# Neighbourhood attention of a two-stack kernel: the column mask built into the shifted bias table by its transfers, in place of an addition on GpSimd

## The reference, cut to what matters

```python
def neighborhood_attn(q, k, v, rpb):          # rpb (H=4, 15, 31)
    rows = s // GRID_W                        # 256 positions = 4 rows x 64 columns
    kh = min(NA_KH_MAX, rows)                 # 4: every query sees all 4 rows
    scores = einsum(q, k) * d ** -0.5
    c0 = clip(c - NA_KW // 2, 0, GRID_W - NA_KW)          # NA_KW = 16
    col_ok = (c[None, :] >= c0[:, None]) & (c[None, :] < c0[:, None] + NA_KW)
    dc = clip(c[None, :] - c[:, None], -15, 15) + 15
    bias = rpb[:, dr][..., dc]
    scores = where(col_ok, scores + bias, NEG_INF)
    p = softmax(scores)
    return einsum(p, v)
```

## Time and profile before

| what | value |
|---|---|
| median of 3 runs | 1360.22 us (1356.76 to 1361.85) |
| the profiled execution's own time | 1358.29 us |
| its span in the profile | 1356.4 us |
| TensorE busy | 1298.9 us, 96% |
| VectorE busy | 989.3 us, 73% |
| ScalarE busy | 696.6 us, 51% |
| GpSimd busy | 279.2 us, 21% |
| DMA, mean share of 16 engines | 56% |
| TensorE's mean granted clock | 0.992 |

### The profile page before, as it was taken

One profiled execution on the slowest core, in us unless ns is written; L12 is line 12 of the kernel. 1 busy time (PEld: TensorE's weight loads), 2 busy tenths in 40 slices (PEclk: granted clock), 3 DMA queues, 4 the chain that ended last, 5 costly groups with the idle time before them and its releaser, 6 DMA issues.

```text
span 1356.4 us, 21347 instructions
## 1 busy us (share of the span) xinstructions
PE 1298.9 (96%) x8100; PEld 1156.5 (85%) x8100; DVE 989.3 (73%) x1172; ACT 696.6 (51%) x952; POOL 279.2 (21%) x253
## 2 busy tenths in 40 slices
PE   3989999998999999999999999999999999999997
PEld 3988898987888888998888888888889898888886
DVE  2697769778776677866766777866776876776776
ACT  3476556645444459554544445444447664544443
POOL 2465247437100012311000005500002410100000
PEclk9999999998999999999999999999999999999999
DMA  8843374355666655424666665766655434666661
GB/s 228 237 157 125 125 208 135 125 152 158 199 188 187 186 156 155 124 95 124 204 190 191 189 184 154 206 190 191 188 158 154 128 111 123 182 191 186 186 190 57
DMA packets 273070, 224.38 MB, mean 165 GB/s; under 512 B 17780, under 2 KB 255735, under 8 KB 272870
## 3 DMA queue, kind: packets, MB, share of 16 engines
q1 hardware_dynamic: 268448, 217.08, 53.5%
q10 hardware_dynamic: 3958, 4.27, 1.0%
q0 software_dynamic: 592, 2.04, 0.9%
HBM read 222.25 MB, written 3.08 MB: 166 GB/s over the span
## 4 chain that ended last, share of the span: by engine, by line
PE 80%; DVE 10%; issue 3%; ACT 3%; DMA 2%; POOL 0%; ACTq 0%; DVEq 0%; POOLq 0%; SPq 0%
PE wide L1550 24%; PE wide L1551 12%; PE big L1513 8%; PE big L1515 8%; PE big L1514 7%; PE wide L1513 5%; PE wide L1514 5%; PE wide L1515 5%; DVE w_lo L833 3%; PE wide L1804 2%; DMA w_raw<-in_w_in 1%; PE wide L1657 1%; ACT w_hi L441 1%; DVE work L1033 1%; DVE proj L889 1%
## 5 line engine op out<-in xcount | busy, mean ns | idle before, releaser
L833 DVE TENSOR_TENSOR w_lo<-w_raw,w_hi 128x2048 fp32r<-128x2048 f32 x205 | 487.3, 2378 | 101.2 <-ACT w_hi L441 100.3
L1550 PE MATMUL wide<-h_both,w_hi 128*128 128x512 f32 x1408 | 500.8, 400 | 0.0
L441 ACT ACTIVATE w_hi<-w_raw 128x2048 fp32r<-128x2048 f32 x206 | 393.6, 1911 | 201.8 <-PE big L1515 133.1
L1551 PE MATMUL wide<-h_both,w_lo 128*128 128x256 f32 x1408 | 396.2, 281 | 0.0
L1550 PEld LDWEIGHTS wide<-h_both,w_hi 128*128 128x128 f32 x1408 | 265.7, 189 | 65.6 <-DVE w_lo L833 0.2
L1551 PEld LDWEIGHTS wide<-h_both,w_lo 128*128 128x128 f32 x1408 | 267.0, 190 | 1.4
L1513 PE MATMUL wide<-h_both,w_hi 128*128 128x256 f32 x720 | 210.2, 292 | 10.0 <-DVE w_lo L833 6.3
L1514 PE MATMUL wide<-h_both,w_hi 128*128 128x256 f32 x720 | 205.4, 285 | 0.0
L1515 PE MATMUL wide<-h_both,w_lo 128*128 128x256 f32 x720 | 205.2, 285 | 0.0
L1513 PE MATMUL big<-w_hi,y_hi 128*128 128x512 f32 x480 | 190.3, 396 | 0.0
L1515 PE MATMUL big<-w_hi,y_lo 128*128 128x512 f32 x480 | 187.8, 391 | 0.0
(11 more groups left out here) (235 smaller groups left out, 1520.9 us busy)
## 6 DMA issues: line engine op xcount, KB each, us to landing
w_raw<-in_w_in SPq DMA_DIRECT2D x112, 512.0 KB, 4.7
w_raw<-in_ffn_w_gate SPq DMA_DIRECT2D x88, 512.0 KB, 4.0
w_raw<-in_ffn_w_up SPq DMA_DIRECT2D x88, 512.0 KB, 5.2
w_raw<-in_ffn_w_down SPq DMA_DIRECT2D x88, 512.0 KB, 4.2
w_raw<-in_w_out SPq DMA_DIRECT2D x32, 512.0 KB, 4.3
work<-rpb_shifted SPq DMA_DIRECT2D x32, 64.0 KB, 4.2
rpb_shifted<-rpb_rows POOLq DMA_DIRECT2D x1, 1920.0 KB, 25.9
cst<-in_consts ACTq DMA_DIRECT2D x1, 1063.0 KB, 6.9
```

The source lines that it names most:

```text
L441: nc.scalar.activation(w_hi[:, r, :], w_raw[:, r, :], ACT.Copy).then_inc(hi_ready, 1)
L833: v.tensor_tensor(w_lo[:, r, :], w_raw[:, r, :], w_hi[:, r, :].bitcast(F32), ALU.subtract).then_inc(lo_ready, 1)
L1550: t_.matmul(o, a_hi, h_both[:, kt].rearrange("p a s -> p (a s)"), start=first, stop=False, skip_group_check=True)
L1551: return t_.matmul(o[:, 0:S], a_lo, h_hi[:, kt, :], start=False, stop=last, skip_group_check=True)
```

## The change

The padded table gets two rows ("variants") of 128 numbers for each of the 120 raw rows, filled with the large negative number in place of zero. Variant 0 holds only the 16 middle numbers of the raw row, variant 1 all 31. The shifted table is then built by five transfers in place of one: the 49 middle query columns come from variant 0, so that their 16-wide window is surrounded by the negative number; for the first 8 and the last 7 query columns the 16 key columns of the window come from variant 1 and the other 48 from a piece of padding. Together the five write the same 1,966,080 bytes. GpSimd's addition L1422 and its two waits go, the mask's 64 columns leave the constants, and VectorE waits for the landing of the 16 transfers of its layer (`bias_in`) itself.

```diff
@@ constants()
-    col = np.arange(P) % GRID_W
-    c0 = np.clip(col - NA_KW // 2, 0, GRID_W - NA_KW)[:, None]
-    kc = np.arange(GRID_W)[None, :]
-    c[:, C_NA:C_NA + GRID_W] = np.where((kc >= c0) & (kc < c0 + NA_KW), 0.0, NEG)
@@ stacks_kernel()
-        padded = y_f[0:DEPTH * NH * RPB_ROWS, 0:P]
+        padded = y_f[0:DEPTH * NH * RPB_ROWS, 0:2 * P].rearrange("n (a c) -> n a c", a=2)
-        scratch = nc.dram_tensor("rpb_rows", (DEPTH * NH * RPB_ROWS, P), F32)
+        scratch = nc.dram_tensor("rpb_rows", (DEPTH * NH * RPB_ROWS, 2, P), F32)
@@ VectorE
-                            dve.wait_ge(bias_ready, l + 1)
+                            dve.wait_ge(bias_in, l * 256 + 256)
                             soft(un, u, na_bias[:, u - 2])
@@ GpSimd
-            link(g.memset(padded, 0.0))
-            pool.dma_start(padded[:, 48:48 + RPB_COLS],
-                           a["na_rpb"].rearrange("l h r c -> (l h r) c")).then_inc(rpb_a, 16)
-            pool.wait_ge(rpb_a, 16)
+            half = NA_KW // 2
+            table = a["na_rpb"].rearrange("l h r c -> (l h r) c")
+            link(g.memset(padded, NEG))
+            pool.dma_start(padded[:, 0, 63 - half:63 + half], table[:, RPB_COLS // 2 - half:RPB_COLS // 2 + half]).then_inc(rpb_a, 16)
+            pool.dma_start(padded[:, 1, 48:48 + RPB_COLS], table).then_inc(rpb_a, 16)
+            pool.wait_ge(rpb_a, 32)
             pool.dma_start(scratch.ap(), padded).then_inc(rpb_b, 16)
             pool.wait_ge(rpb_b, 16)
 
-            pool.dma_start(shifted, bass.AP(scratch, 63, [[P, DEPTH * NH * RPB_ROWS], [-1, GRID_W], [1, GRID_W]])
-                           ).then_inc(rpb_a, 16)
+            def band(at, step, rows_, cols):
+                return bass.AP(scratch, at, [[2 * P, DEPTH * NH * RPB_ROWS], [step, rows_], [1, cols]])
+
+            right, last = GRID_W - half + 1, GRID_W - NA_KW
+            for dst, src in (
+                    (shifted[:, half:right, :], band(63 - half, -1, right - half, GRID_W)),
+                    (shifted[:, 0:half, 0:NA_KW], band(P + 63, -1, half, NA_KW)),
+                    (shifted[:, 0:half, NA_KW:], band(0, 0, half, last)),
+                    (shifted[:, right:, last:], band(P + 63 - right + last, -1, half - 1, NA_KW)),
+                    (shifted[:, right:, 0:last], band(0, 0, half - 1, last))):
+                pool.dma_start(dst, src).then_inc(rpb_a, 16)
             norm(0)
...
-            pool.wait_ge(rpb_a, 32)
+            pool.wait_ge(rpb_a, 16 * 7)
             pool.sem_inc(shifted_ready, 1)
...
                     if (c, j) == (0, DVE_TAPS):
-                        pool.wait_ge(bias_in, l * 256 + 256)
-                        nb = na_bias.rearrange("p t h (a b) -> p (t h a) b", b=GRID_W)
-                        g.tensor_tensor(nb, nb, cst[:, C_NA:C_NA + GRID_W].unsqueeze(1).to_broadcast([P, 32, GRID_W]),
-                                        ALU.add).then_inc(bias_ready, 1)
                         pool.wait_ge(conv_part, l + 1)
                         pool.sem_inc(pool_step, 1)
```

More of the change, by code:

```diff
@@ L93 @@
 B_A, B_L1M, B_C1, B_KS, B_ALL = 8, 12, 16, 20, 24
-C_ID, C_ROT1, C_SWAP, C_ROT2, C_COS, C_SIN, C_SWA, C_FOX, C_DIL, C_NA, C_FREQ, C_FXB, NCONST = (
-    0, 128, 256, 384, 512, 768, 1024, 1536, 2048, 2560, 2624, 2626, 2638)
+C_ID, C_ROT1, C_SWAP, C_ROT2, C_COS, C_SIN, C_SWA, C_FOX, C_DIL, C_FREQ, C_FXB, NCONST = (
+    0, 128, 256, 384, 512, 768, 1024, 1536, 2048, 2560, 2562, 2574)
 FXR = 16
@@ L267, in stacks_kernel @@
         bias_in = sem("bias_in")
-        bias_ready = sem("bias_ready")
         par_T = sem("par_T")
```

## The result

| | before | after |
|---|---|---|
| median | 1359.61 us (1356.76 to 1361.85, 6 runs) | 1350.04 us (1349.21 to 1350.76, 6 runs) |
| ratio, with 95% interval | | 0.9926 (0.9916 to 0.9936) |
| the profiled execution's own time | 1358.29 us | 1350.72 us |
| its span | 1356.4 us | 1348.8 us |
| TensorE busy | 1298.9 us | 1296.3 us |

The change is faster by 0.74%, some 10 us. I had forecast 1.9 us less and called a gain above 0.5% a case of 1 in 10: the forecast, its range (1353.5 to 1365.5) and its chances were wrong. The two profiled executions are 7.6 us apart.

A forecast was written before the change was run, and what follows sets the result against it. It took VectorE as the limit early on, with TensorE waiting behind it. Gains of 2.4 + 1.7 + 0.35 = 4.4 us less 2.5 us for the transfers gave 1.9 us less, 1358.3 us; range 1353.5 to 1365.5 us.

The forecast's parts named there:

- The price of the addition: Both layers: GpSimd's mask addition stalls VectorE's subtraction, 6.66 in place of 2.28 us; removal gives VectorE 4.4 us back.
- 2.4 + 1.7: First layer, TensorE at unit 2: 2.4 us of waiting for exponentials goes, and 1.7 us of low clock behind it.
- In the second layer only 0.35 us of waiting stand at this place: Second layer, TensorE's wait at the same place: removal gains only 0.35 us, though VectorE gains 4.4 us there too.
- fourth rival: Whole kernel: earlier work escapes further low-clock stretches, two on top of the whole 4.4 us, giving 1352.5 us; chance 0.10.
- The new transfers: Start of the kernel: the five table transfers cost 2.5 us, 1.7 for more pieces plus 0.8 for another issue.
- what the table takes longer I count in full: Start: a later table delays the weights that VectorE's chain hangs on, so all of 1.7 + 0.8 us counts.
- A line through both has 14.9 ns for a piece and the rest for its bytes: Table transfers at the start: piece price from two queues' shares, making 1800 more pieces 1.7 us of every engine.
- The scratch doubles to 120 KB, but in as many pieces; I put that at nothing: Scratch at the start: 60 KB more are 0.2 us at 264 GB/s, so counted as nothing.
- below, it may be nothing or 1 us of gain: Start: lower bound of the transfers' cost, if short pieces spread the load of the engines better.
- the second rival: Start: tables dealt to 15 engines in place of 16, landing at 34.1 us, 9.0 us lost, 1364.8 us; chance 0.17.
- the transfers cost nothing: Start: time goes with bytes, which stay the same, so the 4.4 us come whole, 1355.8 us; chance 0.20.
- The gain not taken: Behind the exponentials another wait ends as late, so only the start's 2.5 us loss remains, 1362.7 us; chance 0.08.

The follow-up runs named there:

- no_mask: Kernel before with only GpSimd's mask addition taken away, so the bias goes unmasked and the table is built as before: 1353.59 us, ratio 0.9956.
- scratch_144: Kernel before with scratch rows 576 bytes apart in place of 512, table still one transfer of 7680 rows: 1354.3 us (1 run).
- changed_again: The changed kernel run once more, nothing altered: 1349.99 us, ratio 0.9921 against the kernel before.
- by_layer: Changed kernel with the second layer's tables built during the first layer by five more transfers: 1350.34 us, ratio 0.9925 against the kernel before.
- scratch_doubled: Kernel before with scratch rows 1024 bytes apart in place of 512, table still one transfer of 7680 rows: 1369.73 us (1 run).
- two_of_3840: Kernel before with its table built by two transfers of 3840 rows in place of one of 7680: 1352.95 us (1 run).
- the last variants: Changed kernel with the two scratch variants in separate blocks, rows 512 or 576 bytes apart: 1349.81 and 1349.13 us.
- transfers_only: Changed kernel with the mask addition and the mask's constants put back: 1356.41 us, ratio 0.9971 against the kernel before.

## Why the prediction was wrong

**The price of the addition: right in mechanism, and right in size for the first layer.** "The subtraction has stood still behind the addition": 6.66 us became 2.28, and with the addition put back into the changed kernel it is 6.67 again. "2.4 + 1.7" for the first layer was 4.1, and `no_mask` measured 4.06. The Trainium skill's page "SBUF — State Buffer", section "SBUF: two separate sides", has a shared port pair that a GpSimd operation, or a VectorE operation with two inputs in SBUF against a GpSimd one that reads SBUF, holds for the whole instruction if it starts first, while the other is fully blocked. The traces agree: the addition started 0.05 us ahead, and 2.1 us are left from its end to the subtraction's.

**The second layer: undersized.** The step "In the second layer only 0.35 us of waiting stand at this place" took one wait as the whole effect. It measured 2.07 us. The low clock at 230 to 234 us stood in the trace before, and ended some 16 us ahead of the wait that I read (249.1 us); it had made TensorE late by itself. A wait is what is left after both sides' delays; where the side that waits has been slowed too, the wait is a lower bound. The prediction's fourth rival (the clock gives more, 0.10) named this kind of thing, and its 1352.5 us was the nearest of the five numbers, but it named no place.

**The new transfers: wrong sign, the main error.** The term said +2.5 us. Measured on the mark of GpSimd's first operation it is -4.0 us, and in time -3.9 us. The failed step is the one from the engines' time to the delay: "what the table takes longer I count in full", with the 25.9 us of the landing taken as what these bytes and pieces need in any form. The engines' time was nearly the same, 22.1% for q0 against 21.6%, 0.3 us of every engine more, and the table was still done 6.0 us earlier (33.2 against 39.2 us), because the tail of few packets was gone.

The price of a piece, "A line through both has 14.9 ns for a piece and the rest for its bytes", was worked out from a share that held 99 slow packets, so it isn't a price of small pieces as such. With the 13.8% of the same 7680 pieces in `scratch_144` the same formula gives 0.138 x 16 x 55 / 7920 = 15.3 ns for 258 bytes in place of 24.0, the line through that and the 46.6 ns for 898 bytes has 2.7 ns for a piece, and the 1.7 us of the term become 0.3. Neither is what the runs show for 1800 more pieces at a like form, 1.8 us at 512 bytes and 0.8 at 576. And no such price gives the right sign: with 0.3 in place of 1.7 the term is still +1.1 us.

"The scratch doubles to 120 KB, but in as many pieces; I put that at nothing": with the one transfer it cost 9.3 us of time (1369.73 against 1360.48 us beside it, one run, whose profiled start is 10.0 us later at the convolution), more than any other single edit here moved the time. In the change its harm was outweighed by the split into five.

What I did see right was whom it would hit: "what the table takes longer I count in full", on SyncE's hanging issue. The same path carried the gain: 12.12 us of hanging became 2.98. And the sentence "below, it may be nothing or 1 us of gain" set the lower bound too narrow. The table's 25.9 us called for a bound of its own on this side: had it landed in half the time, up to 12 us of a hanging issue would have come free. I only weighed slower forms for it (the second rival: 34.1 us), never a quicker one.

**The rivals.** That the transfers cost nothing (0.20) fell on the good side of it: they gave. That the table goes to fewer engines (0.17) fell by its own condition: the packets under way level off at 15 in the kernel before as after, so nothing changed there. The Trainium skill's page "DMA: Bandwidth & Descriptors", section "Why a DMA increments its semaphore by 16 and not by 1", takes the largest number up to 16 that divides the outermost counts of both sides. The packets agree: before, the destination has 7680 rows but the source 120, which gives 15. That the change would move it from 16 to 15 was my misreading, since I took the destination alone. The estimate of 6.5 us from that page's section "Anatomy of one DMA" still isn't reached: the quickest form of all 1920 KB in one transfer took 12.6 us. The gain not taken (0.08) was wrong.

**Where the profile's 7.6 us stand to this.** The removal's 4.1 and 2.1 us of `no_mask` and the start's 4.0 would be 10.2 in all, near the medians' 9.6, but no single profile shows that sum. In the profiled execution of the changed kernel the first layer gave only 1.73 of its 4.06 us. TensorE came to unit 0 earlier than VectorE and ScalarE did, waited 2.1 and not 1.5 us, and the low clock at 92 to 97 us followed. That isn't chance of one execution: the profile of `changed_again` has the same stretch at 0.66 and the same span, 1348.8 us. So part of the start's gain is given back inside the first layer, as in `by_layer`. The 2.0 us between the profiles' 7.6 and the medians' 9.6 are the 1.3 us by which the profiled execution of before was faster than its median and the 0.7 by which that of the changed kernel was slower.

**By the list of what would show it.** The subtraction at 2.3 us: came true. The wait before unit 2 and its low clock gone: came true. Unit 0's wait "stays near 1.5 us but lies 2 to 3 us later, because the weights of slot 4 land at 50 to 51 us": wrong, ScalarE takes the same weights up at 43.72 us where it was 48.05. The text said that the start's part would be wrong if the half slot's issue ended before 39.8 us, and it did, at 31.1 us.

**What stays open.** Why the packets of one form of transfer slow down, and why a few of them make a tail. The distance between the rows read matters (576 bytes against 512 against 1024), the split matters, and the distance of the tables written matters in the one transfer (25.9 to 12.6 us) but not in the five (13.4 to 13.5). The records of the packets name no engine and no place in memory. A rival is untested: `scratch_144` and `scratch_doubled` also make the scratch longer, so the tables behind it may have begun at another address, and no run moves them with the distance kept. `two_of_3840` shows only that the addresses of before don't by themselves make the table slow. Whether the 1 to 2 us between the spans of the last variants are real is open too.

## What to carry to other kernels

When a transfer from DRAM to DRAM takes much longer than its bytes, count it as a fault that an innocent edit may mend or worsen, and put the mended case into the range; here 64 bytes more between the rows read took the landing from 25.9 to 12.7 us. Its share of the engines doesn't tell its delay (21.6% and 22.1% here, done at 39.2 and 33.2 us): look at when its last packet ends, and at whose issue hangs while it is under way, since that is where the time comes back. And a short wait behind a stretch of low clock is a lower bound of what its cause costs: compare the length of the whole stretch between two marks, not the wait.

## What was unexpected in the hardware

- The landing of a table of 1920 KB from DRAM to DRAM in 256-byte pieces went from 12.7 to 25.9 to 37.2 us as the rows read lay 576, 512 and 1024 bytes apart, with the same pieces and the same 4096-byte packets; the packets over 0.6 us were 15, 99 and 138.
- Splitting the same pieces into two or five transfers took the landing to 11.2 us for each half and 10.0 us for the largest of five, and the table was done at 27.3 and 26.7 us in place of 39.2, with more issue time on GpSimd (five issues: 5.67 us, one: 2.80).
- The table's packets took as much of the engines before as in the changed kernel (11.6 and 11.7 us of each), but the last one ended 22.1 us after the first in the one and 14.9 us in the other.
- The same wait of 1.8 us on TensorE was followed by a stretch at 0.62 of the clock in one kernel (before, 230 to 234 us) and, at the same place of `transfers_only`, by none (1.14 us for the scores there, 1.67 in before).
